# Expert stage of a diffusion step: first couple gathered from four token tiles, nine weight homes

## The reference, cut to what matters

```python
h2 = rms_norm(x, norm2_g) * (1 + scale2) + shift2
g_idx  = top_1(h2 @ w_grp + b_grp)                       # one group of 4
top_i  = top_2((h2 @ w_exp + b_exp)[group])              # two of its 4 experts
combine = softmax(top_v) * g_p
for e in range(16):
    he = silu(h2 @ w1[e]) * (h2 @ w3[e])                 # 1024 -> 512
    y  = y + combine[:, e:e + 1] * (he @ w2[e])          # 512 -> 1024
x = x + gate2 * y
```

## Time and profile before

| | |
|---|---|
| median of 3 runs | 1188.54 us (1188.28 to 1190.12) |
| the profiled execution | 1188.92 us |
| its span in the profile | 1187.1 us |
| TensorE busy | 1135.3 us, 96% of the span |
| DVE, ACT, POOL busy | 48%, 19%, 33% |
| moved by DMA | 200.88 MB, of it 185.20 MB on SP's queue |
| mean granted TensorE clock | 0.985 |

### The profile page before, as it was taken

The page is one execution under the profiler, slowest core; times in us unless marked ns, Lnnn a source line. Parts: engine busy times, 40 slices in busy tenths (PEclk is TensorE's granted clock), DMA queues, the critical chain, the costliest instruction groups (busy, mean ns, idle before and its releaser), DMA issues.

```text
span 1187.1 us, 15083 instructions
## 1 busy us (share of the span) xinstructions
PE 1135.3 (96%) x5942; PEld 718.2 (61%) x5943; DVE 569.9 (48%) x1114; ACT 229.2 (19%) x492; POOL 391.7 (33%) x345
## 2 busy tenths in 40 slices
PE   3999999999999999999999999999979999999995
PEld 1667777777777777777777777755544333333432
DVE  3554478455796695385444445636672121211121
ACT  4222356122571002001100010001121011111000
POOL 1475500469004444345444444100011133222222
PEclk9999999999999999999999999999969999999998
DMA  9955120022200222222212226441169999999972
GB/s 353 340 200 192 45 80 1 18 71 80 81 1 1 72 71 72 71 71 71 71 71 71 71 71 230 178 159 54 71 255 404 414 405 413 395 412 405 398 298 29
DMA packets 54007, 200.88 MB, mean 169 GB/s; under 512 B 5616, under 2 KB 6192, under 8 KB 47792
## 3 DMA queue, kind: packets, MB, share of 16 engines
q1 hardware_dynamic: 47056, 185.20, 40.4%
q0 software_dynamic: 6272, 13.13, 4.3%
q10 hardware_dynamic: 608, 1.58, 0.3%
HBM read 189.36 MB, written 18.91 MB: 175 GB/s over the span
## 4 chain that ended last, share of the span: by engine, by line
PE 87%; DMA 8%; DVE 3%; SPq 1%; issue 0%; ACT 0%; POOLq 0%; POOL 0%; DVEq 0%
PE psum L2375 30%; PE psum L2158 12%; PE psum L2575 6%; PE psum L2462 5%; PE psum L2394 4%; DMA weight_ring<-in_w 4%; PE psum L2279 4%; PE psum L2135 4%; PE psum L2339 3%; DMA arena<-in_w 2%; PE psum L2651 2%; PE psum L2637 2%; PE psum L2599 2%; PE psum L2577 2%; PE psum L2083 2%; PE psum L2313 1%
## 5 line engine op out<-in xcount | busy, mean ns | idle before, releaser
L2375 PE MATMUL psum<-arena,weight_ring 128*128 128x320 f32 x864 | 238.7, 432 | 0.0
L808 POOL TENSOR_TENSOR weight_ring<-weight_ring 128x512 f32<-128x512 f32 x80 | 105.1, 1314 | 300.3 <-PE psum L2375 123.2
L2375 PEld LDWEIGHTS psum<-arena,weight_ring 128*128 128x128 f32 x864 | 163.1, 190 | 65.6
L2375 PE MATMUL psum<-x,weight_ring 128*128 128x320 f32 x480 | 133.1, 432 | 0.0
L2375 PEld LDWEIGHTS psum<-x,weight_ring 128*128 128x128 f32 x480 | 90.7, 190 | 37.0
L809 POOL TENSOR_TENSOR weight_ring<-weight_ring 128x512 f32<-128x512 f32 x80 | 110.8, 1385 | 0.0
L2158 PE MATMUL psum<-weight_ring,x 128*128 128x256 f32 x384 | 88.0, 380 | 0.0
L2575 PE MATMUL psum<-weight_ring,arena 128*32 128x512 f32 x512 | 77.3, 593 | 3.2 <-DMA weight_ring<-in_w 2.1
L2158 PEld LDWEIGHTS psum<-weight_ring,x 128*128 128x128 f32 x384 | 71.7, 190 | 11.3 <-issue 1.9
L1616 DVE TENSOR_TENSOR arena<-psum,arena 128x320 f32<-128x320 f32 x96 | 45.7, 487 | 59.2 <-PE psum L2375 58.6
L2462 PE MATMUL psum<-weight_ring,arena 128*128 128x512 f32 x160 | 72.0, 597 | 0.5 <-DVE arena L1682 0.5
(11 more groups left out here) (360 smaller groups left out, 1730.1 us busy)
## 6 DMA issues: line engine op xcount, KB each, us to landing
arena<-in_w SPq DMA_DIRECT2D x22, 2048.0 KB, 19.7
weight_ring<-in_w SPq DMA_DIRECT2D x21, 2048.0 KB, 24.7
weight_ring<-in_w_in SPq DMA_DIRECT2D x15, 2048.0 KB, 8.5
arena<-in_w_ada SPq DMA_DIRECT2D x6, 2048.0 KB, 13.0
x<-in_w SPq DMA_DIRECT2D x5, 2048.0 KB, 24.9
x<-in_x_sample SPq DMA_DIRECT2D x2, 2048.0 KB, 12.2
arena<-in_w_ada SPq DMA_DIRECT2D x4, 1024.0 KB, 14.4
weight_ring<-in_w_ada SPq DMA_DIRECT2D x4, 1024.0 KB, 14.3
```

What stands on the lines that cost most here:

```text
L808: nc.gpsimd.tensor_tensor(out[:, 0:2], a_[:, 0:2], b_[:, 0:2], op)
L2375: last = mm(out, w[:, k, :], src[:, k, :], start=(k == 0), stop=(k == 3))
```

## The change

- The first main tile gets 64 slots of a and 64 of b (`main_lanes`), the first half tile 32 of a, 32 of b and 64 of couple 1's b (`half_lanes`). The main tile's rows come from the latent tiles 0 to 3 alone: `first_places`, `first_hots`, `first_table` and `first_slots` make its index in `idxc` before tile 4 is routed, and POOL gathers it once four tiles of h2 are stored. The full table is made later, in the middle of the gate product of couple 0, and the weight table after up 0; gather 1 and 2 wait for the full table and the last tile's store.
- `place_rules` gets the split of couple 0 and runs after the last tile's `choose`; `choose` takes a function between its two experts. DVE takes over half of POOL's product for the last tile. `wide_hots` has five buffers in place of two.
- `keep_busy` multiplies the identity by itself, 512 columns at a time: once before the last router part, five times before the first tokens.
- Six and three weight homes become one ring of nine (`homes`) in the order of release (`freed_in_order`). No load waits for a gather; couple 0's six and couple 1's first two go out early. In the last couple down b is loaded ahead of up a.
- The add of main tile 0 is in two parts of 64 rows, that of half tile 0 in three (32, 32, 64). POOL issues each next gather ahead of the adds, not behind them.
- The late rows' transpose follows half gate and up 0; ACT copies tokens 0 ahead of the late rows.

```diff
+def matrices(t):
+
+    if t + 1 == COUPLES:
+        return [(part, which, t) for part, which in (("gate", "b"), ("up", "b"), ("gate", "a"), ("down", "b"), ("up", "a"), ("down", "a"))]
+    return [(part, which, t) for part in ("gate", "up", "down") for which in "ab"]
+
+
+def freed_in_order():
+
+    freed = [(part, which, 0) for part in ("gate", "up") for which in "ab"]
+    for t in range(1, COUPLES - 1):
+        freed += [("gate", "a", t), ("up", "a", t), ("gate", "b", t), ("up", "b", t), ("down", "a", t)]
+        if t == 1:
+            freed.append(("down", "a", 0))
+        if t % 2:
+            freed += [("down", "b", t - 1), ("down", "b", t)]
+    return freed
+
+
+HOMES = 9
+LOADS = [name for t in range(COUPLES) for name in matrices(t)]
+HELD_BY = dict(zip(LOADS[HOMES:], freed_in_order()))
+HOME = {}
+for _n, _name in enumerate(LOADS):
+    HOME[_name] = _n if _n < HOMES else HOME[HELD_BY[_name]]
+
+
+def load_count(name):
+
+    return sum(HOME[other] == HOME[name] for other in LOADS[:LOADS.index(name) + 1])
 
 
...
 
-ADDS = sum(2 if t < WHOLE else 1 for t in range(COUPLES)) + 2 * QUADS
+def main_lanes(t):
+
+    return ((0, 64, "a"), (64, P, "b")) if t == 0 else ((0, 32, "a"), (32, 64, "a"), (64, 96, "a"), (96, P, "b"))
+
+
+def half_lanes(j):
+
+    first = ((0, 32, "a", 0), (32, LANE, "b", 0)) if j == 0 else ((0, LANE, "b", 2 * j),)
+    return first + ((LANE, P, "b", 2 * j + 1),)
+
+
...
+            def last_use(name):
+                part, which, t = name
+                if part == "down":
+                    sp.wait_ge(s_d, 2 * (out_main(t) if which == "a" and t else out_half(t // 2)) + 2)
+                elif which == "b" or t == 0:
+                    sp.wait_ge(s_half_mm, t + 1)
+                else:
+                    sp.wait_ge(s_gate_mm if part == "gate" else s_up_mm, t + 1)
+
+            def load(part, which, t, e):
+                name = (part, which, t)
+                if name in HELD_BY:
+                    last_use(HELD_BY[name])
...
             sp.wait_ge(s_order, 1)
-            for t in range(COUPLES - 1):
+            a, b = expert_at(COUPLES - 1), expert_at(COUPLES)
+            load("gate", "a", 0, a)
+            job_done(sp, "wo", 2 * NT - 1)
+            load("gate", "b", 0, b)
+            load("up", "a", 0, a)
+            sp.wait_ge(s_outx, 16 * CTX)
+            load("up", "b", 0, b)
+            sp.wait_ge(s_x2, 2 * NT)
+            sp.wait_ge(s_last_scaled, 1)
+            load("down", "a", 0, a)
+            sp.wait_ge(s_h2out, 16 * CTX)
+            load("down", "b", 0, b)
+            a, b = expert_at(COUPLES - 2), expert_at(COUPLES + 1)
+            sp.wait_ge(s_late, 1)
+            load("gate", "a", 1, a)
+            load("gate", "b", 1, b)
+            sp.wait_ge(s_wtable, NT)
+            load("up", "a", 1, a)
+            load("up", "b", 1, b)
+            load("down", "a", 1, a)
+            load("down", "b", 1, b)
+            for t in range(2, COUPLES):
                 a, b = expert_at(COUPLES - 1 - t), expert_at(COUPLES + t)
-                if t == 1:
-                    sp.wait_ge(s_late, 1)
-                if t >= 2:
-                    sp.wait_ge(s_half_mm, t - 1)
-                load_gate_up("gate", "a", t, a)
-                if t == 0:
-                    job_done(sp, "wo", 2 * NT - 1)
-                load_gate_up("gate", "b", t, b)
-                if t:
-                    sp.wait_ge(s_gate_mm, t)
-                load_gate_up("up", "a", t, a)
-                if t:
-                    sp.wait_ge(s_up_mm, t)
-                else:
-                    sp.wait_ge(s_xg[0], 16)
-                    sp.wait_ge(s_outx, 16 * NT)
-                load_gate_up("up", "b", t, b)
-                if t == 0:
-                    sp.wait_ge(s_x2, 2 * NT)
-                    sp.wait_ge(s_last_scaled, 1)
-                elif t == 1:
...
-            for half in range(2):
-                pool.wait_ge(s_x2, 2 * CTX + half + 1)
-                part = slice(512 * half, 512 * (half + 1))
-                nc.gpsimd.tensor_tensor(gate1[:, 0, part], x_sb[:, D * CTX:D * NT][:, part], mod2[:, 0, 1, part], mult).then_inc(s_last_wide, 1)
+            pool.wait_ge(s_x2, 2 * CTX + 1)
+            nc.gpsimd.tensor_tensor(gate1[:, 0, 0:512], x_sb[:, D * CTX:D * CTX + 512], mod2[:, 0, 1, 0:512], mult).then_inc(s_last_wide, 1)
 
             pool.wait_ge(s_slot, 1)
-            pool.wait_ge(s_h2out, 16 * NT)
+            pool.wait_ge(s_h2out, 16 * CTX)
+            gather(0, idxc[:, 0:1], s_xg[0], N_LAT)
+            pool.wait_ge(s_slot, 2)
+            pool.wait_ge(s_last_h2out, 16)
 
             added = [0]
 
@@ -938,21 +936,25 @@
                     pool.wait_ge(s_T, n - XG + 1)
                     gather(n % XG, idx_row[:, TOKEN_TILES[n]:TOKEN_TILES[n] + 1], s_xg[n % XG])
 
-            for n in range(XG):
+            for n in range(1, XG):
                 gather(n, idx_row[:, TOKEN_TILES[n]:TOKEN_TILES[n] + 1], s_xg[n])
...
             def add_half(j):
                 c = COUPLES + j
-                add_rows(out_half(j), 0, LANE, idx_row[0:LANE, c:c + 1], idx_ctx[0:LANE, c:c + 1])
+                if j == 0:
+                    add_rows(out_half(j), 0, 32, idx_row[0:32, c:c + 1], idx_ctx[0:32, c:c + 1])
+                    add_rows(out_half(j), 32, LANE, idx_b[0:32, 0:1], idx_b_ctx[0:32, 0:1])
+                else:
+                    add_rows(out_half(j), 0, LANE, idx_row[0:LANE, c:c + 1], idx_ctx[0:LANE, c:c + 1])
                 add_rows(out_half(j), LANE, P, idx_q[0:LANE, j:j + 1], idx_q_ctx[0:LANE, j:j + 1])
 
             for t in range(COUPLES - 1):
+                gather_next(XG + 2 + out_main(t))
                 add_main(t)
-                gather_next(XG + 2 + out_main(t))
                 if t % 2:
+                    gather_next(XG + 2 + out_half(t // 2))
                     add_half(t // 2)
-                    gather_next(XG + 2 + out_half(t // 2))
             add_half(QUADS - 1)
             add_main(COUPLES - 1)
...
+            def first_slots():
+                dve.wait_ge(s_table, 1)
+                V.tensor_scalar(idxc[:, 0:1], first_psum, float(EMPTY), None, add).then_inc(s_slot, 1)
...
             ranks(NT - 2)
             expert_order()
             residual(2 * NT - 1)
+            dve.wait_ge(s_x2, 2 * NT)
+            V.tensor_tensor(gate1[:, 0, 512:D], x_sb[:, D * CTX + 512:D * NT], mod2[:, 0, 1, 512:D], mult).then_inc(s_last_wide, 1)
             rank_distance()
             x2_sum(NT - 1)
-            place_rules()
+            first_places()
             x2_rstd(NT - 1)
             dve.sem_inc(s_last_rstd, 1)
-            choose(NT - 1)
+            first_hots()
+            choose(NT - 1, first_slots)
             dve.wait_ge(s_last_scaled, 1)
             h2_shifted(NT - 1)
+            place_rules()
             rules_found()
             ranks(NT - 1)
             places()
@@ -1920,9 +1966,9 @@
             link(V.scalar_tensor_tensor(out=whole, in0=e_exp, scalar=1.0, in1=gsum, op0=add, op1=mult))
             link(V.reciprocal(comb[:, 0:NT], whole))
             link(V.tensor_tensor(comb[:, NT:2 * NT], comb[:, 0:NT], e_exp, mult))
...
+            def first_table(part):
+                pe.wait_ge(s_hot, part + 1)
+                for n in range(CTX * part, CTX * (part + 1)):
+                    last = mm(first_psum, first_hot[:, n, :], pair_vals[:, n // 2:n // 2 + 1], start=(n == 0), stop=(n == 2 * CTX - 1))
+                return last
+
             ps = open_job("route", NT - 1)
             route_part(NT - 1, ps, 0)
-            x2_T(2 * NT - 1)
-            route_part(NT - 1, ps, 1).then_inc(s_job, 1)
             pe.wait_ge(s_w[LATE_SLOT[0]], 32)
             pe.wait_ge(s_w[LATE_SLOT[1]], 32)
             ada_part(LAST_PAIR, late_psum, range(0, 1), late_slot)
+            x2_T(2 * NT - 1)
+            keep_busy(1, 1)
+            route_part(NT - 1, ps, 1).then_inc(s_job, 1)
+            ada_part(LAST_PAIR, late_psum, range(1, 2), late_slot)
+            first_table(0)
+            ada_part(LAST_PAIR, late_psum, range(2, 3), late_slot)
+            first_table(1).then_inc(s_table, 1)
+            ada_part(LAST_PAIR, late_psum, range(3, ADA_STEPS), late_slot).then_inc(s_late, 1)
             rank(NT - 1)
             count(NT)
-            ada_part(LAST_PAIR, late_psum, range(1, 2), late_slot)
-            for i in range(NT):
-                table(i)
-            ada_part(LAST_PAIR, late_psum, range(2, ADA_STEPS), late_slot).then_inc(s_late, 1)
-            emptied(pe, INDEX[("rank", NT - 1)])
+            keep_busy(5, 1)
+            emptied(pe, INDEX[("route", NT - 1)])
...
+            next_tokens(0)
+            pe.wait_ge(s_xgT, TOKEN_TILES.index(0) + 1)
+            main_part(0, "gate", gate_psum, range(0, KT - NT))
+            for i in range(NT):
+                last = main_part(0, "gate", gate_psum, range(KT - NT + i, KT - NT + i + 1))
+                if i == NT - 1:
```

(19 more changed lines are left out.)

257 lines of the change are left out of this document (127 added, 130 removed).

## The result

The changed kernel takes 1190.88 us in the median of 10 executions (1188.43 to 1192.92), the kernel before, beside it, 1187.95 us (10, 1186.76 to 1190.41). The ratio is 1.0019, with a 95% interval of 1.001 to 1.0027: slower by about 2.2 us (the two medians lie 2.9 apart), where I had forecast a fall of 0.6, too small to be told from no change. The profiled execution took 1190.28 us, its span is 1188.5 us.

A forecast was written before the change was run, and what follows sets the result against it. TensorE was taken as the bound almost everywhere after 893 us, the weight stream right behind. main_down(0) 3.6 us later less 4.2 us of weight waits gives -0.6 against 1188.92; the median, 0.4 lower, makes 1188.0 us, range 1183.5 to 1192.

The forecast's parts named there:

- separate term for the clock: Transposes and start of couple 0's gate: TensorE's clock may fall while idle, losing 0 to 3.4 us; 1.0 taken.
- the added wait: Couple 0, before half_down: ACT copies and stores the late rows ahead of silu_half(0), costing another 0.5 us.
- within 0.2%: Whole kernel: no change that can be told, 1186.2 to 1190.5 us; chance 0.40.
- the 874.5 to 877.5 given as a sign: POOL, before the expert stage: first gather issued in this span (us) and landing in 11 to 14 us.
- Step 1: Last tile's routing: early index on DVE and TensorE, choose starting at 870.7, index ready at 874.5 us (873.6 to 876.5).
- The fourth matrix: Start of the weight stream: fourth weight matrix, issued at 868 with the others, lands at 893 us and no longer matters.
- The weight waits vanish: Expert stage: TensorE's 4.2 us of waits for weight matrices disappear behind a TensorE 3.6 us late.
- step 4: Weight stream: 4.0 us of DMA idle goes, 0 to 2 lost again; awaited matrices come 2 to 4 us earlier.
- The slower rival: Expert stage: POOL's serial scatter-adds hold up the end, +4.5 us, 1193.4; chance 0.24, shared with a low clock.
- low clock in both places: Index products before the first gather, and couple 0's start: both at 1.2 GHz; part of the slower 0.24.
- The faster rival: Up to main_down(0): clock holds, index at 873.6, gather landing 887.0, change -2.6 to -5.7, 1183 to 1186 us; chance 0.36.
- It doesn't do what it says: First gather: lands after 890 because first_table ran at low clock; +1.4, 1190 us; mostly inside the 0.40.

The follow-up runs named there:

- the hold: Changed kernel, with loads from couple 0's up b onward waiting again for the first gathered rows; ratio 1.0026 to the kernel before.
- the pick in the gap: Changed kernel, with pick_lanes moved from ahead of up 0 to behind the transposes of tokens 1, during ACT's copy; ratio 1.0018 to the kernel before.
- no scratch products: Changed kernel without the five identity products before the first tokens (the single earlier one stays); ratio 1.0026 to the kernel before.
- the run with eleven products: Changed kernel with eleven identity products instead of five before the first tokens; median 1189.14 us of 12, ratio 1.0014 to the kernel before.
- the combination: Changed kernel, slot tables before tokens 0, pick_lanes during the tokens 1 copy, more scratch products around the tables; ratio 0.9966 (five executions), run again 0.9992 (twelve).
- the tables first and the pick: Changed kernel, slot tables before tokens 0 and pick_lanes during the tokens 1 copy, five scratch products as they were; ratio 0.9990 to the kernel before.
- the late gather: Changed kernel, slot tables before tokens 0, later weight loads held, first gather from the full index after the last store; 1192.75 us, ratio 1.0045.

## Why the prediction was wrong, and where it was right

main_down(0) was forecast to end at 931.9 and ended at 934.16. The steps between, forecast and measured:

| step | forecast | measured |
|---|---|---|
| first gather lands | 888.0 | 886.9 |
| to the start of the gate product | 2.1 | 3.2 |
| gate, tables, pick_lanes | 10.3 | 13.7 |
| separate term for the clock | 1.0 | (in the two lines above) |
| up | 7.0 | 7.0 |
| weight table and shifts | 5.0 | 3.9 |
| transposes of tokens 1, then wait or gap | 1.6 | 2.2 |
| half gate/up | 7.0 | 7.1 |
| from there to down, with the added wait | 2.9 | 3.0 |
| down | 7.0 | 7.0 |
| main_down(0) ends | 931.9 | 934.2 |

**The step that failed is the clock's term.** "Between 0 and 3.4 I take 1.0", said the prediction. The transposes lost 1.94 less 1.05 = 0.9 us, the first 16 instructions of the gate 6.15 less 3.65 = 2.5, together 3.4: the upper end to the tenth. That it is the very end is partly chance: the transposes took 1.94 us in four profiles with gaps of 4.8 to 11.1 us ahead of them, but the 16 instructions behind them 6.15 (the kernel after), 6.00 (the hold), 5.20 (the pick in the gap) and 5.11 (no scratch products), so that the loss is 2.4 to 3.4 us. None of them is near 1.0. The 1.0 was a value between "it holds" and "it falls", while the rows spoke for the upper end: seven idle us in one piece were forecast, and the earlier trace rows had a mean of 0.62 from 867 to 894, with 7.8 idle us in all. A term with two levels has to be taken at one of them. With 3.4 the sum would have been +6.0 − 4.2 = +1.8, and the forecast about 1190.3 us, slower and not faster; the profile's difference was +1.4 (1190.28 less 1188.92). This term alone turns the sign of the sum. The median, 1190.88, lies above the 1190.5 at which "within 0.2%" ends, and inside the whole range to 1192. In the six executions of the run with eleven products in which the clock was 0.992 or more, the time is 1187.5 us, 0.4 below the kernel before: about the forecast.

The Trainium skill, "TensorE: Matmul & The Clock Gate", section "What's actually happening", says that the gate isn't aligned with the kernel, so that the number of matmuls run at the lower clock differs from run to run. The runs here agree: one kernel, the combination, gave executions of mean clock 0.985 to 0.995, 1181.6 to 1194.6 us.

**Smaller misses that cancelled.** Not counted: the copy of tokens 1 ahead of the half gate/up (1.16 us; the wait of 0.5 for the second gather, which I had put in that place, didn't come, as its 9.5 us to landing were hidden), and that gate products cut by tables run 1.01 us a piece and the tables 0.55, together some 0.9 us over the sum. Too high: the weight table, 3.4 for 4.5, since its five groups no longer wait for DVE between them, and the landing (1.1 us early; the residual ended 0.9 us earlier in this execution). These are +2.1 and −2.7 us; 0.4 is rounding and the wait behind the late rows, 0.8 for 0.5.

**Right.** The landing of the first gather, 886.9 for 888.0, but by two errors against each other: it was issued at 873.4, 2.0 us before the 875.4 of the sum and outside the 874.5 to 877.5 given as a sign, and took 13.5 us, not 12.5. (Step 1 also adds ten operations of 0.2 and two of 0.3 to 2.4; they make 2.6.) The fourth matrix no longer matters, and goes out at 867.7. The added wait behind the late rows is there (L2678, 0.8 us). **The weight waits vanish**, all 4.2 us, and further gain was small (0.7 us). But not for the reason in step 4, matrices that come 2 to 4 us earlier. Stretches of the kernels before and after, and of the combination run again:

```profile
866.00:932.00 66.00, 56.62 (x399) 26.30 (x403) 30.84 (x132) 11.56 (x19) 7.46 (x8) 0.84 0.93 374
...
866.00:932.00 66.00, 56.67 (x307) 27.89 (x307) 29.19 (x145) 10.53 (x17) 5.26 (x6) 0.87 0.92 370
...
866.00:932.00 66.00, 61.88 (x382) 29.61 (x385) 28.90 (x144) 10.32 (x17) 7.35 (x8) 0.97 1.01 419
```

Up to 932 us the DMA engines of the kernel after have moved no more than before (370 against 374 GB/s): the tenth load goes out at 914.3, the next, behind half_gate_up(0), at 924.2, and the share of 0.57 from 920 to 930 is 4.3 idle us, not 0 to 2. The lead of the start is gone, and what is left against the waits is a TensorE that is 5.9 us late.

**The rivals.** In the kernel after the adds never stopped TensorE. The timeline of POOL:

```profile
953.56 1.48 POOL L926 DMA_INDIRECT y_sample<-arena,slot_rows  x1 [19.07 <-DVE arena L2062]
...
964.59 1.41 POOL L926 DMA_INDIRECT y_sample<-arena,slot_rows_q  x1 [7.82 <-DMA y_sample<-arena,slot_rows]
...
974.63 1.47 POOL L926 DMA_INDIRECT y_sample<-arena,slot_rows  x1 [4.26 <-DMA y_sample<-arena,slot_rows_q]
```

The first add came at 953.6 (near 948 forecast): the late rows were stored 2.1 us later than forecast, and gate2 was used at 948.8, not 945.6. The two steps shown are 11.0 and 10.0 us, that of couple 1's 96 rows is 15.2 (14.5 for couple 2's in the kernel before), those of the three adds of half 0 are 12.4, 7.8 and 10.4, and couple 2's first add starts at 1028.4 (1025 forecast). DVE waits for the adds a great deal:

```profile
DVE arena L2054 <- DMA y_prompt<-arena,slot_rows_b_ctx: 76.7, 5, 22.0
DVE arena L2054 <- DMA y_prompt<-arena,slot_rows_q_ctx: 34.9, 4, 12.4
```

But TensorE's own list has no wait behind it, so these 111.6 us cost nothing here. It is a near thing: half_down of couples 4 and 5 starts at 1101.4, and the first half of DVE's rows, which empties its PSUM bank, is made at about 1101.2 (an estimate: L2062 starts at 1100.5 and takes 0.7 a half). In three of the variants above TensorE comes there earlier and does wait, 0.5 us with the pick in the gap, 0.5 without scratch products and 0.9 with the tables first and the pick. The slower rival's mechanism is real, then, and caps what such edits gain. Within that rival the case "low clock in both places" is what came, though the first place cost the path nothing, and had too little of the 0.24. The faster rival's index and landing came too (887.0 forecast, 886.9 measured), without its clock. "It doesn't do what it says" fell: the gather is as early as planned.

**What stays open.** Which part of the change removed the weight waits is settled in part. The delay of main_down(0) alone isn't it: in the combination run again main_down(0) ends at 926.0, 2.3 us earlier than in the kernel before, and TensorE waits for no matrix; there the stream is ahead at 932 us (419 against 374 GB/s). Nor is the early stream alone: with the queue held, and with the late gather too, no wait came back, and there main_down(0) ends at 935.0 and 934.8, with 366 GB/s up to 932 in both. An estimate from these numbers (what was moved up to 932 us more or less than before, at 405 GB/s, and the end of main_down(0)) has TensorE some 5 us further behind the stream than before in each of these three kernels and in the kernel after, more than the 4.2 of waits. The ring of nine alone in the kernel before was not tried, so the share of its order isn't known.

## What to carry to other kernels

When a change opens an idle gap on TensorE ahead of dense work, price the clock near its full loss; even with scratch products up to 1.4 us from the tokens it held in only half of the executions here. Look first for real work to put into the gap: here five small tables moved into it were worth 2.3 us by the ratios. Work that was pulled forward is paid by what must then follow the start; count both sides up to one fixed event, here main_down(0), and then ask how much waiting behind that event there is to give back, and which chain is next: here POOL's adds, 0.2 us behind. Before a wait in a trace is laid to an edit, look whether it lies behind the place where the edit acts. Where one kernel's executions differ by a clock that holds or falls, take a dozen of them before believing a gain of 0.3%.

## What the runs showed of the hardware, unexpected

- The kernels with scratch products up to the tokens have executions that fall into two groups by their mean granted clock, 3.7 us apart in one kernel (eleven products) and 4.7 in another (the combination). Of the kernel after, with products that end 6 us before the tokens, none of ten executions had a mean clock above 0.990.
- The first gather, of 128 rows of 4 KB, landed between 886.7 and 887.0 us in five kernels that issued it at 873.0 to 874.0, behind three or six weight loads alike; issued at 874.5 and 874.6 in two others it landed at 887.6 and 887.4. Issued at 886.8 into a DMA system with a share of 0.31 (886 to 890) it took 4.4 us.
- DMA engines at a share of 0.57 for 10 us, with TensorE 5.9 us later than before, left no trace in TensorE's waits for weights.
